# Two-layer hybrid encoder on one core: gathering the experts' tokens with an indirect DMA and transposes, with changes around the gate products, the head norms and the last expert

## The reference

```
logits = (h @ router)
probs = softmax(logits);  top_p, top_i = top_k(probs, 2);  top_p /= sum(top_p)
gates[s, e] = top_p if e in top_i else 0
out = sum over e of gates[:, e:e+1] * (silu(h @ w_gate[e]) * (h @ w_up[e])) @ w_down[e]
```

## Time and profile before

| | |
|---|---|
| median of 3 runs | 1707.84 us (1707.12 to 1708.0) |
| the profiled execution | 1706.54 us |
| its span, first to last instruction | 1704.7 us |
| PE busy | 1666.4 us, 98% of the span |
| DVE, ACT, POOL busy | 1251.1, 989.0, 76.2 us |
| chain that ended last, share of PE | 97% |
| granted TensorE clock, mean | 0.986 of 2.4 GHz |
| experts | 8, from about 692 us to the end |

### The profile page before, as it was taken

One profiled execution on the slowest core, in us unless ns is written; L12 is line 12 of the kernel. 1 busy time (PEld: TensorE's weight loads), 2 busy tenths in 40 slices (PEclk: granted clock), 3 DMA queues, 4 the chain that ended last, 5 costly groups with the idle time before them and its releaser, 6 DMA issues.

```text
span 1704.7 us, 22510 instructions
## 1 busy us (share of the span) xinstructions
PE 1666.4 (98%) x8656; PEld 1377.6 (81%) x8656; DVE 1251.1 (73%) x1197; ACT 989.0 (58%) x958; POOL 76.2 (4%) x94
## 2 busy tenths in 40 slices
PE   7999999999999999899999999999999999999997
PEld 3868995999988886688888888888888888888886
DVE  5578555544423673788988988988898988988985
ACT  2356333433433432677677677676776777777773
POOL 2005230000000030000000000000000000000000
PEclk9999999999989999899999999999999999999999
DMA  6411014555433211899999999999999999999992
GB/s 242 113 43 49 2 50 148 165 181 198 173 125 122 100 50 50 311 371 367 332 372 367 329 364 374 318 378 371 331 363 370 326 369 349 351 375 337 351 375 97
DMA packets 199502, 428.77 MB, mean 252 GB/s; under 512 B 10746, under 2 KB 34574, under 8 KB 199438
## 3 DMA queue, kind: packets, MB, share of 16 engines
q1 hardware_dynamic: 199438, 427.90, 69.9%
HBM read 426.82 MB, written 1.05 MB: 251 GB/s over the span
## 4 chain that ended last, share of the span: by engine, by line
PE 97%; DVE 1%; ACT 1%; issue 0%; DMA 0%; SPq 0%; DVEq 0%; ACTq 0%
PE bank L2658 18%; PE bank L2660 18%; PE bank L2659 18%; PE bank L2442 5%; PE bank L2374 4%; PE bank L2373 4%; PE bank L2375 4%; PE bank L1962 3%; PE bank L1949 2%; PE bank L2667 2%; PE bank L2139 2%; PE bank L2601 2%; PE bank L2343 2%; PE bank L2162 2%; PE bank L2703 1%; PE bank L2519 1%
## 5 line engine op out<-in xcount | busy, mean ns | idle before, releaser
L1895 DVE TENSOR_TENSOR split<-ring,split 128x2048 fp32r<-128x2048 f32 x336 | 764.0, 2290 | 112.9 <-ACT split L1114 109.6
L1114 ACT ACTIVATE split<-ring 128x2048 fp32r<-128x2048 f32 x336 | 640.3, 1924 | 175.4 <-PE bank L2660 173.7
L2658 PE MATMUL bank<-split 128*128 128x512 f32 x896 | 354.4, 396 | 2.6 <-DVE split L1869 1.4
L2660 PE MATMUL bank<-split 128*128 128x512 f32 x896 | 349.1, 390 | 0.0
L2659 PE MATMUL bank<-split 128*128 128x512 f32 x896 | 348.8, 389 | 0.0
L2658 PEld LDWEIGHTS bank<-split 128*128 128x128 f32 x896 | 168.3, 188 | 36.3 <-issue 1.6
L2660 PEld LDWEIGHTS bank<-split 128*128 128x128 f32 x896 | 168.1, 188 | 36.0
L2659 PEld LDWEIGHTS bank<-split 128*128 128x128 f32 x896 | 168.5, 188 | 33.2
L2658 PE MATMUL bank<-split,ehr_ 128*128 128x512 f32 x448 | 180.6, 403 | 0.0
L2660 PE MATMUL bank<-split,ehr_ 128*128 128x512 f32 x448 | 174.8, 390 | 0.0
L2659 PE MATMUL bank<-split,ehr_ 128*128 128x512 f32 x448 | 174.7, 390 | 0.0
(11 more groups left out here) (475 smaller groups left out, 1984.2 us busy)
## 6 DMA issues: line engine op xcount, KB each, us to landing
ring<-in_od_moe_gate SPq DMA_DIRECT2D x112, 1024.0 KB, 6.9
ring<-in_od_moe_up SPq DMA_DIRECT2D x112, 1024.0 KB, 7.3
ring<-in_od_moe_down SPq DMA_DIRECT2D x112, 1024.0 KB, 6.7
ring<-in_od_w_in SPq DMA_DIRECT2D x7, 2048.0 KB, 7.7
ring<-in_ev_w_in SPq DMA_DIRECT2D x6, 2048.0 KB, 9.0
ring<-in_ev_ffn_gate SPq DMA_DIRECT2D x11, 1024.0 KB, 5.3
ring<-in_ev_ffn_up SPq DMA_DIRECT2D x11, 1024.0 KB, 7.9
ring<-in_ev_ffn_down SPq DMA_DIRECT2D x5, 2048.0 KB, 7.8
```

The source lines that it names most:

```text
L1114: act.activation(wst[:, r % NSTAGE, 0, :], ring[:, (r % NHALF) * HALF:(r % NHALF + 1) * HALF], ACT.Copy).then_inc(w_hi, 1)
L1895: dve.tensor_tensor(wst[:, r % NSTAGE, 1, :], ring[:, (r % NHALF) * HALF:(r % NHALF + 1) * HALF], wst[:, r % NSTAGE, 0, :].bitcast(F32), S ...
L2658: pe.matmul(o, hi, wh, start=start, stop=False)
L2660: return pe.matmul(o, lo, wh, start=False, stop=stop)
```

## The change

- `xn` is written to DRAM once, as rows (`xrows`, POOL, in expert 0). For the next expert PE multiplies `sel` with a column of token numbers (`next_rows`, behind up(1)), DVE copies the 128 numbers to `row_of` (duty "rows", ahead of r = 10), POOL fetches these rows with an indirect DMA into `xtok`, and PE turns them with 8 transposes (`turn_rows`, behind up(6)). Only expert 0's tokens are still gathered by matmul. `select` moves from r = 20 to r = 6.
- down(5) is split: first half, turn(6), second half. DVE's scaling of the tokens (duty "tokens") moves ahead of r = 0, the split ("tokens_split") stays ahead of r = 1.
- The last expert stands in the program by itself on PE, with no next tokens; its down(6) finishes bank 4 first and then bank 5, and the combine of each bank follows by itself, into banks 6, 7, 0, 1.
- The 16 gate products are spread, one behind each matmul of `od_pair(0)`. `norm(2)` gets two matmuls whose result nobody reads, 512 and 256 columns.
- `kinv` and `head_row` have 128 partitions, zero below the eighth, and the matmuls on them contract over 128 rows.
- SP waits for the stores behind the flag's branch, not ahead of it. Three semaphores of constants become one (`dve_const`).

```
-        head_row = sb("head_row", [HA, 4, P])
-        kinv = sb("kinv", [HA, SEQ])
+        head_row = sb("head_row", [P, 4, P])
+        kinv = sb("kinv", [P, SEQ])
...
-        duties[1].append(("tokens", 0))
+        duties[0].append(("tokens", 0))
+        duties[1].append(("tokens_split", 0))
         duties[2].append(("result", 0))
         duties[5].append(("gates", 0))
-        duties[20].append(("select", 0))
+        duties[6].append(("select", 0))
+        duties[10].append(("rows", 0))
...
+        LAST_BANK = (6, 7, 0, 1)
...
-                    sp.wait_ge(stored, 64 * (ps + 1))
...
                 with sp.If(sp.value_load(flag[0:1, 0:1], min_val=0, max_val=1) > 0):
+                    sp.wait_ge(stored, 64)
                     expert_pass(1)
                     store(1)
+                    sp.wait_ge(stored, 128)
+                sp.wait_ge(stored, 64)
...
+                def fetch_rows(ps):
+
+                    for e in range(NE):
+                        pool.wait_ge(ix_rdy, NE * ps + e + 1)
+                        pool.indirect_dma_start(xtok, None, xrows, bass.IndirectOffsetOnAxis(row_of[:, 0:1], 0)
+                                                ).then_inc(rows_moved, 16)
+                    pool.wait_ge(rows_moved, 16 * (TT + NE * (ps + 1)))
+
+                pool.wait_ge(xn_rdy, TT * 4)
+                pool.wait_ge(eh_rdy, 1)
+                for a in range(TT):
+                    pool.dma_start(xrows[P * a:P * a + P, :], xn[:, a, :]).then_inc(rows_moved, 16)
+                pool.wait_ge(rows_moved, 16 * TT)
+                fetch_rows(0)
...
+                        elif what == "rows":
+                            dve.wait_ge(ix_ps, i + (at + NE * ps + 1))
+                            dve.tensor_copy(row_of[:, 0:1], B[7][:, 0:1]).then_inc(ix_rdy, 1)
...
+                    low_result(ps, NE - 1, 0)
+                    combine(ps, NE - 1, e, 0, LAST_BANK[0])
+                    low_result(ps, NE - 1, 1)
+                    for q in range(1, 4):
+                        combine(ps, NE - 1, e, q, LAST_BANK[q])
...
+                if ni == 2:
+                    for n in (512, 256):
+                        pe.matmul(B[4][:, 0:n], ident[:, :], smask[:, 0].rearrange("p m s -> p (m s)")[:, 0:n],
+                                  start=True, stop=True)
...
+                            if t == 0 and (f, k) < (1, KT - 1):
+                                gate_product(f, k)
...
-                                         ident[0:HA, j:j + 1].to_broadcast([HA, P]), kinv[:, :], start=True, stop=True)
+                                         ident[:, j:j + 1].to_broadcast([P, P]), kinv[:, :], start=True, stop=True)
...
+                def next_rows(ps, i, at):
+
+                    pe.wait_ge(sel_rdy, i + (at + (NE + 1) * ps + 2))
+                    for a in range(TT):
+                        last = pe.matmul(B[7][:, 0:1], sel[:, a, :], tokc[:, a:a + 1], start=(a == 0), stop=(a == TT - 1))
+                    last.then_inc(ix_ps, 1)
+
+                def turn_rows(ps, i, at):
+
+                    pe.wait_ge(rows_moved, i * 16 + 16 * (TT + at + NE * ps + 1))
+                    for k in range(KT):
+                        last = pe.transpose(B[1 + 2 * (k // 4)][:, P * (k % 4):P * (k % 4) + P],
+                                            xtok[:, P * k:P * k + P], ident[:, :])
+                        if k % 4 == 3:
+                            last.then_inc(xg_ps, 1)
...
+                def down_halves(j):
+
+                    pe.wait_ge(ht_lo, i * NC_E + (NC_E * (at + NE * ps) + 1 + j))
+                    pe.wait_ge(w_lo, i * PER + (PER * (at + NE * ps) + PER))
+                    for n in range(2):
+                        for h in range(2):
...
                         project("up", j)
-                        if j:
+                        if j == 1:
+                            next_rows(ps, i, at)
+                        if 0 < j < NC_E - 1:
                             down(j - 1)
+                    if not last_one:
+                        turn_rows(ps, i, at)
+                    down(NC_E - 2, (0,))
                     turn(NC_E - 1)
-                    gather(ps, i, at + 1)
-                    down(NC_E - 1)
+                    down(NC_E - 2, (1,))
+                    if last_one:
+                        down_halves(NC_E - 1)
+                    else:
+                        down(NC_E - 1)
```

More of the change, by code:

```diff
@@ L54 @@
     "sin_rdy qk_std kk_std ln1_std ln0_std ba_sb sp_l ge_rdy on_std rt_exp".split())}
+DVE_CONST = {n: i + 1 for i, n in enumerate("eps cols mask".split())}
 DVE_STEPS = {n: i + 1 for i, n in enumerate(
@@ L307, in hybrid_trunk @@
         cntf = sm.take(1)
+        tokc = sm.take(TT)
         landed = [sem(f"landed{i}") for i in range(NSTAT)]
@@ L1087, in duty @@
                     def duty(what, j):
-                        if what == "tokens":
+                        if what == "tokens_split":
                             for r in range(2):
@@ L1872, in duty @@
                             if at:
-                                low_result(ps, i)
+                                for n in range(2):
+                                    low_result(ps, i, n)
                         elif what == "gates":
                             if at:
-                                combine(ps, i, bass.ds(i, 1))
+                                for q in range(4):
+                                    combine(ps, i, bass.ds(i, 1), q, 4 + q)
                         elif what == "select":
@@ L2428, in _, with gate_product @@
                 pe.wait_ge(x_rdy, 8)
-                for a in range(TT):
-                    for k in range(KT):
-                        last = pe.matmul(B[2][:, 16 * a:16 * a + 16], hT[:, k, P * a:P * a + P], ba_w[:, k, :],
-                                         start=(k == 0), stop=(k == KT - 1))
-                last.then_inc(pe_step, 1)
+                def gate_product(a, k):
+                    last = pe.matmul(B[2][:, 16 * a:16 * a + 16], hT[:, k, P * a:P * a + P], ba_w[:, k, :],
+                                     start=(k == 0), stop=(k == KT - 1))
+                    if a == TT - 1 and k == KT - 1:
+                        last.then_inc(pe_step, 1)
                 def od_pair(t):
@@ L2705, in turn, with down @@
                         last.then_inc(ht_ps, 1)
-                    def down(j):
-                        pe.wait_ge(ht_lo, i * NC_E + (NC_E * (at + NE * ps) + 1 + j))
-                        for h in range(2):
+                    def down(j, halves=(0, 1)):
+                        if 0 in halves:
+                            pe.wait_ge(ht_lo, i * NC_E + (NC_E * (at + NE * ps) + 1 + j))
+                        for h in halves:
                             r = at_half["down", j, h]
@@ L2718, in down @@
                             last.then_inc(half_ps, 1)
+                    def down_halves(j):
+                        pe.wait_ge(ht_lo, i * NC_E + (NC_E * (at + NE * ps) + 1 + j))
+                        pe.wait_ge(w_lo, i * PER + (PER * (at + NE * ps) + PER))
+                        for n in range(2):
+                            for h in range(2):
+                                for k in range(2):
+                                    last = product(B[4 + n][:, :], ehs[:, j % 2, 0, 2 * h + k, :],
+                                                   ehs[:, j % 2, 1, 2 * h + k, :], at_half["down", j, h],
+                                                   slice(D * k + 512 * n, D * k + 512 * n + 512),
+                                                   False, h == 1 and k == 1)
+                            last.then_inc(half_ps, 1)
                     for j in range(NC_E):
@@ L2742, in all_experts @@
                     expert(ps, 0, 0)
-                    with pe.Fori(0, NE - 1) as i:
+                    with pe.Fori(0, NE - 2) as i:
                         expert(ps, i, 1)
-                    combine(ps, NE - 1, 0)
+                    expert(ps, NE - 2, 1, last_one=True)
+                    combine(ps, NE - 1, 0, LAST_BANK)
                 pe.sem_inc(half_ps, NSTAGE)
```

88 lines of the change are left out of this document (49 added, 39 removed).

## The result

The changed kernel takes 1697.99 us (median; 1695.93 to 1699.07), the kernel before on the same chip 1706.2 us. The ratio is 0.9946, 95% interval [0.9934, 0.9959]. I had forecast 1692 with a range of 1684 to 1705, against a profiled 1706.54. The sign is right and the range holds the time, but of the 15.6 us forecast only 8 (by the medians) to 9 (by the ratio) are there. The profiled execution of after took 1699.07 us, its span is 1697.4 us (before: 1704.7).

What follows compares the result with a forecast made beforehand. PE was taken as the bound, busy for all 124.00 us of an expert. Terms -1.7 - 1.1 + 0.8 - 1.3 - 2.6 - 3.4 - 3.4 - 2.9 = -15.6 from 1706.54 gave 1690.9, forecast as a median of 1692, range 1684 to 1705.

Steps and rivals of the forecast that it cites:

- the first rival: PE's new 1.95 us wait ahead of down(6) drops the clock; one to four falls give 1695 to 1706, chance 0.20.
- The boundary: End of each expert, gather replaced by turned rows: new wait of 1.95 us ahead of down(6), 0.67 us gained an expert.
- The 22.5 us that the counted matmuls promise: Gathers replaced or dropped, counted alone as 7 x 2.70 + 3.57 us; the prediction itself did not believe it.
- The index product: Two new one-column fp32 matmuls on PE in every expert, costing 0.42 us, at the high end 0.9.
- Tokens ahead of r = 0: DVE scales the gathered tokens before its product r = 0; a loss of 0.8 us in expert 0, none in steady state.
- The fetch: Index copy and row transfer hidden under over 90 us of expert work: cost 0, uncovered up to 8 us an expert.
- The clock outside the experts: Falls at 85 and 546 us go with 128 rows, -3.4 us each; the stretch at 481 shortens, -2.9 us.
- the idle time stays, so the fall stays: PE's 1.77 us idle at 480 still drops the clock, but it returns halfway, near 488: -2.9 us.
- The tail: After the last matmul, bank 4 completes earlier, so combines and adds end near 1696.4: -1.3 us.
- SP's end: SP reads the flag while the stores fly, so the span ends at 1702.1 in place of 1704.7: -2.6 us.

Runs made afterwards that it cites:

- e1: Changed kernel plus 14 matmuls of 256 columns that nobody reads, filling the wait between down(5) and down(6) of every expert; 1692.72 us, ratio 0.9917.
- e5: Kernel before plus only the 128-row norms, spread gate products with two extra matmuls, and early flag; gather and last expert unchanged; 1693.96 us, ratio 0.9927.
- e2: Changed kernel with the low part of the last turn of products ahead of product r = 41 instead of behind it; 1686.3 us, ratio 0.9882.
- e6: Changed kernel with the turn of the rows moved from ahead of down(5) to right ahead of down(6); 1688.25 us, ratio 0.9888.
- e9: Changed kernel with e2's and e6's orders, the last down's halves reordered and two waits filled at expert 0; 1673.84 us, ratio 0.981.
- e10: e9's kernel with every expert's rows fetched twice to the same place; 1674.81 us, ratio 0.982.
- e3: Changed kernel with head_row and kinv back at 8 rows; 1703.44 us, ratio 0.9978.
- e4: Changed kernel with the 16 gate products together again and without the two matmuls that nobody reads; 1699.81 us, ratio 0.9967.
- e11: Kernel before with e2's one-number edit, the low part of the last turn ahead of product r = 41; 1715.32 us, ratio 1.0057.
- e12: Changed kernel with gate products spread but without the two matmuls that nobody reads ahead of them; 1698.62 us, ratio 0.9964.

## Why the prediction was right in sign and off in size

**The step that failed** is the choice between the forecast and the first rival: "the new wait drops the clock". I gave one to four falls 0.20 on the ground that the 2.01 us in the tail was followed by none. That was weak evidence, one place, with little work behind it. Four falls came, behind waits of 1.83 us. Without them (e1) experts are 123.73 apart and the forecast's 123.8 holds. I also priced a fall at 3.4 us, by those of 6.8 us length; these are 3.4 us long and cost 1.6 to 1.7. Four at the right price are 6.5 us in the trace (5.3 by e1's median), most of the 7.4 us that are missing. At my price four would have given 1705.6, where 1698 was measured. The measured 1698 lies outside the 1687 to 1697 of the forecast itself. The range holds it because it was drawn over this rival.

**The boundary** was sized rightly by the trace of before: wait 1.83 for 1.95, and from the first half of down(5) to down(6) in the last expert 1674.01 to 1681.96, 7.95 for 7.98. The 22.5 us that the counted matmuls promise were rightly not believed. e5 shows that the exchange is worth less than nothing with the falls, and e2 and e6 that one change of order makes it pay; e9 has both. The index product takes 0.36 us of PE an expert (715.69 to 716.05) for 0.42.

**Tokens ahead of r = 0** in expert 0: from the gather's start to the transposes behind gate(0) 692.26 to 706.48 before, 683.49 to 698.62 after, +0.9 for +0.8.

**The fetch** costs 0 (e10). No product on DVE got longer: its mean is 2289 ns, as before.

**The clock outside the experts.** The falls at 85 and 546 went, as forecast; e3 puts 5.5 us on them for 6.8. The stretch at 481: "the idle time stays, so the fall stays" is wrong for the profiled execution, in which all of it is gone, 5.7 us for 2.9 between the traces. e4 gives 1.8 by the medians and 3.6 by the ratios. The kernel before's order shows 13.6 us in one profile and 6.8 in the other (e11, at 484), so the 13.6 us were a long case. Together with the flag these edits were to bring 12.3 us, and e5 measured 11.6.

**The tail**: from the last down matmul's end to the last add 4.1 us in place of 5.5, -1.4 for -1.3. **SP's end**: -1.4 for -2.6 in this execution. The last store, issued by 1692.2, has landed only at 1696.95, 4.8 us behind its issue, and the end follows that. That is a case of its own: in the ten other profiles with this tail (e1 to e4, e6 to e10, e12) the last store lands 2.9 to 3.4 us behind its issue, and the span ends 3.2 to 3.4 us behind the branch and 4.5 to 4.7 behind the last add, near the forecast's 3.0 and 4.4. What held the one store up stays open.

**The balance between the two traces**: -3.5 and -3.7 (falls at 85, 546), -5.7 (gate stretch), +0.9 (expert 0), -2.0 (seven experts at 123.74), +6.5 (four falls), -1.1 (last expert), -1.4 and -1.4 (tail) make -11.4, where the spans differ by -7.3. The other 4.1 lie in places that the change doesn't touch: the clock's first rise came at 18.65 us in place of 13.55 (+1.8), the low stretch at the router was 13.6 us long in place of 10.2 (+1.3), and +1.1 in the feed-forward block of layer 0, which I can't name. The first two differ between executions of like kernels.

**Open**: why only some of the waits of 1.83 us drop the clock. It is not fixed to every second one: of eight waits after and e4 have falls behind the first, third, fifth and seventh, e3 behind the third, fifth and seventh, e12 behind the second, fifth and seventh. Open too is why the last store of after landed late, and where the 1.1 us of the feed-forward block come from.

## What to carry to other kernels

Work taken off the bounding engine is worth only what its successors' operands are early by. If it covered a chain on the others, the gain turns into a wait, and a wait on TensorE can cost its clock on top: here 1.83 us idle plus, about every second time, 1.6 more. So look where the chain's last link is queued (here behind a product of 2.3 us that nobody needed yet) and put the remaining work (here the transposes) under the chain, not ahead of it; if nothing can be moved, matmuls that nobody reads can fill the wait, which kept the clock here and delayed nothing (e1). And an order in a shared table moves on every engine that reads it: the same edit brought 11.7 us in one kernel and cost 8 in the other, by the medians.

## What the runs showed of the hardware

- Behind a PE wait of 1.83 us ahead of down(6) the granted clock fell to 0.50 for 3.4 us in 14 of 32 cases (4 of 8 in after and in e4, 3 of 8 in e3 and in e12), behind one of 1.75 us (e6) it didn't. Behind waits of 0.7 and 0.94 us (seven of each, e2 and e6) it fell in none, behind one of 2.2 us (e2) in the one case there was, and behind the 2.01 us in the tail of before it stayed at 1.00 for the 5.4 us that rows 5 show.
- PE can be busy all the time and lose its clock: with 8 rows in the contraction the falls at 85 and 543 came back (e3), with 128 rows they are gone (after, and e5 in the order of before), at 379 ns a matmul in place of 374.
- One core alone drew 367 and 371 GB/s over 122 us, with no engine waiting for weights.
- An indirect transfer of an expert's rows (0.5 MB) landed 7.3 us after its issue by POOL, in the median of eight (6.6 to 9.3); a plain 1 MB load of an expert's weights by SP took 6.6 to 7.1, by the medians of gate, up and down.
